# A two-block transformer kernel on one core: RMS norms by token on partitions, a weight split moved on VectorE, and a triangular inverse done two chunks at a time

## The reference, cut to what matters

```
def first_block(x, ...):                                   # 256 tokens, D 1024, D_FF 2816
    x = x + 0.5 * swiglu(rms_norm(x, ffn1_norm), ...)
    h = rms_norm(x, mix_norm);  p = h @ w_in
    y_a = rwkv7_mixer(token_shift(p[..., :SHIFT_COLS], mu), ...) @ rwkv_proj
    y_b = fox_mixer(...) @ fox_proj                        # forgetting attention, 8 heads of 64
    x = x + (gate_a * y_a + gate_b * y_b) @ w_out
    x = x + 0.5 * swiglu(rms_norm(x, ffn2_norm), ...)
    return rms_norm(x, final_norm)

def second_block(x, c, ctx, c_ctx, w_ada, ...):
    mod_x, mod_c = silu(c) @ w_ada + b_ada, silu(c_ctx) @ w_ada + b_ada     # 9 x 1024 each
    x   = x   + 0.5 * g1x * swiglu_2(modulate(rmsnorm(x), sh1x, sc1x), ...)
    ctx = ctx + 0.5 * g1c * swiglu_2(modulate(rmsnorm(ctx), sh1c, sc1c), ...)
    # both sets: projections, two-way retention; x: 2D rope, Fourier branch, gates, out
    x = x + g3x * 0.5 * swiglu_2(...)
    return rmsnorm(x, norm_final)
```

## Time and profile before

| | before |
|---|---|
| median of 3 runs | 1769.89 us (1769.77 to 1769.99) |
| the profiled execution | 1771.81 us |
| its span, first to last instruction | 1770.0 us |
| PE busy | 1704.9 us (96%) |
| DVE busy | 1059.6 us (60%) |
| ACT busy | 652.3 us (37%) |
| PE granted clock, mean | 0.991 of full |

### The profile page before, as it was taken

The page is one execution under the profiler, slowest core; times in us unless marked ns, Lnnn a source line. Parts: engine busy times, 40 slices in busy tenths (PEclk is TensorE's granted clock), DMA queues, the critical chain, the costliest instruction groups (busy, mean ns, idle before and its releaser), DMA issues.

```text
span 1770.0 us, 32228 instructions
## 1 busy us (share of the span) xinstructions
PE 1704.9 (96%) x13366; PEld 1552.1 (88%) x13366; DVE 1059.6 (60%) x1570; ACT 652.3 (37%) x763; POOL 5.2 (0%) x13
## 2 busy tenths in 40 slices
PE   6999999899999999999999999899999999999997
PEld 6999898676998999998888888888889799989997
DVE  6766747542766766765465465942356634676766
ACT  4333446222544333432222212522346334443332
POOL 0000000000000000000000000000000000000000
PEclk9999999999999999999999999999999999999999
DMA  6545566476244545422222222232223235445551
GB/s 245 190 175 185 193 257 240 152 283 256 100 165 171 190 168 187 166 85 105 95 95 95 95 95 96 95 119 104 90 96 106 97 143 185 176 151 184 185 190 48
DMA packets 37537, 267.74 MB, mean 151 GB/s; under 512 B 4192, under 2 KB 4448, under 8 KB 5456
## 3 DMA queue, kind: packets, MB, share of 16 engines
q1 hardware_dynamic: 36432, 262.37, 40.8%
q0 software_dynamic: 1024, 4.17, 0.6%
HBM read 265.48 MB, written 1.05 MB: 151 GB/s over the span
## 4 chain that ended last, share of the span: by engine, by line
PE 92%; DVE 4%; ACT 2%; issue 1%; DMA 1%; DVEq 0%; POOL 0%; SPq 0%; ACTq 0%
PE PS L329 25%; PE PS L330 24%; PE PS L331 24%; PE PS L542 2%; PE PS L543 2%; PE PS L544 2%; PE PS L562 2%; PE PS L981 2%; PE PS L407 1%; PE PS L1014 1%; PE PS L1001 1%; ACT W_HI L316 1%; PE PS L783 1%; DVE RSTD L1467 1%; PE PS L968 1%
## 5 line engine op out<-in xcount | busy, mean ns | idle before, releaser
L329 PE MATMUL PS<-H_HI,W_HI 128*128 128x256 f32 (+1 forms) x2128 | 652.0, 306 | 21.0 <-DVE H_LO L1459 11.9
L330 PE MATMUL PS<-H_LO,W_HI 128*128 128x256 f32 (+1 forms) x2128 | 647.0, 304 | 0.0
L331 PE MATMUL PS<-H_HI,W_LO 128*128 128x256 f32 (+1 forms) x2128 | 646.8, 304 | 0.0
L316 ACT ACTIVATE W_HI<-RAW 128x2048 fp32r<-128x2048 f32 x213 | 407.2, 1912 | 585.0 <-PE PS L331 553.9
L324 DVE TENSOR_TENSOR W_LO<-RAW,W_HI 128x2048 fp32r<-128x2048 f32 x213 | 487.3, 2288 | 189.4 <-ACT W_HI L316 188.9
L329 PEld LDWEIGHTS PS<-H_HI,W_HI 128*128 128x128 f32 x2128 | 411.2, 193 | 43.8 <-issue 27.6
L330 PEld LDWEIGHTS PS<-H_LO,W_HI 128*128 128x128 f32 x2128 | 411.5, 193 | 15.4 <-issue 0.2
L331 PEld LDWEIGHTS PS<-H_HI,W_LO 128*128 128x128 f32 x2128 | 411.1, 193 | 14.9
L329 PE MATMUL PS<-HID_HI,W_HI 128*128 128x256 f32 (+1 forms) x704 | 218.4, 310 | 3.3 <-DVE XC L1509 3.3
L330 PE MATMUL PS<-HID_LO,W_HI 128*128 128x256 f32 (+1 forms) x704 | 217.9, 309 | 0.0
L331 PE MATMUL PS<-HID_HI,W_LO 128*128 128x256 f32 (+1 forms) x704 | 217.8, 309 | 0.0
(11 more groups left out here) (315 smaller groups left out, 1713.8 us busy)
## 6 DMA issues: line engine op xcount, KB each, us to landing
RAW<-stream SPq DMA_DIRECT2D x249, 1024.0 KB, 4.8
XC<-xin SPq DMA_DIRECT2D x2, 512.0 KB, 5.0
XC<-xin POOLq DMA_DIRECT2D x1, 1024.0 KB, 5.1
out<-NT POOLq DMA_DIRECT2D x2, 512.0 KB, 2.9
CON<-consts POOLq DMA_DIRECT2D x1, 548.0 KB, 6.0
LW<-lora POOLq DMA_DIRECT2D x1, 512.0 KB, 6.6
DFT<-dft POOLq DMA_DIRECT2D x1, 512.0 KB, 3.8
ROPE<-rope POOLq DMA_DIRECT2D x1, 256.0 KB, 3.4
```

What stands on the lines that cost most here:

```text
L316: nc.scalar.activation(W_HI[s % RING][:], RAW[u % RING][:], ACT.Copy).then_inc(hi_done, 1)
L329: nc.tensor.matmul(acc, w_hi, x_hi, start=first, stop=False)
L330: nc.tensor.matmul(acc, w_hi, x_lo, start=False, stop=False)
L331: return nc.tensor.matmul(acc, w_lo, x_hi, start=False, stop=last)
```

## The change

1. **Norms.** The squares become the stationary operand (tokens on the result's partitions) and a two-column constant `ONE3` the moving one, so the sums are 128x2. The root and the reciprocal are of 128x2, and `norm_spread` brings the reciprocals back to every partition with a matmul against the identity; DVE scales from PSUM. All eight tiles are scaled first, and then all are subtracted. PE's first unit takes the high activations first (`two`), and the low ones behind. `nd` and `ne` share one pass over the squares: a second column of weights `SQW` gives the sum for the norm behind the norm.
2. **Order on DVE.** `split_lo(s0 + 34)` leaves the end of the FFN: it goes behind the additions, in two halves, or, ahead of the FFN of both sets, ahead of the reciprocals of `nd`. The first norm's low split moves between the scaling and the subtraction.
3. **PE fill.** Seven matmuls at the start, and three to five around the norms `na`, `nc` and `ni` (`keep_clock`), compute nothing that is used.
4. **The end of the FFN of both sets** is done by set: eight tiles of the main set, eight of the context, each 256 columns wide instead of eight of 512. The norm `ng` runs beside the context's tiles.
5. **The inverse in pairs of chunks.** The odd chunk of a pair has its heads' halves crossed, so it uses the two 64x64 tiles off the diagonal. One `z_step` and one `x_step` stand for two. In `x_step` the products with `ZM` on the left stay on the diagonal for both chunks, and those of the odd chunk wait for a semaphore `x_cross`. `products` of odd chunks has another order. `ada(12)` ahead becomes `ada(16)`, twenty `ada(4)` become ten `ada(8)`, and `ada(12)` ahead of `fox_qk` becomes two times `ada(4)`.
6. The output is stored by SP in four pieces instead of by GpSimd in two.

`three` also takes the high, the low and again the high weights instead of high, high, low. That leaves the number of matmuls and weight loads as it is.

How the change moves the instructions stands here at two places, engine by engine in program order.

```diff
-ADA_INV = 23
-ADA_AFTER = {PHASE["fox_qk"] - 1: 3, PHASE["fox_v"] + 1: ADA_INV}
+ADA_INV = 24
...
+            o = slice(0, UNIT) if part is None else slice(part * UNIT // 2, (part + 1) * UNIT // 2)
+            last = nc.vector.tensor_tensor(W_LO[s % RING][:, o], RAW[u % RING][:, o], W_HI[s % RING][:, o].bitcast(F32), ALU.subtract)
+            if part != 0:
+                last.then_inc(lo_done, 1)
...
-                last = nc.tensor.matmul(NORM_BANK[name], con("ones"), tmp[:, k], start=(k == 0), stop=(k == 7))
-                if k == 7:
+                w = 4 if name == "nd" else 2
+                for tt in range(2):
+                    last = nc.tensor.matmul(sums(name), tmp[:, k, tt * P:(tt + 1) * P], SQW[:, k, 2 - 2 * tt:6 - 2 * tt] if w == 4 else
...
+            def keep_clock(n, bank):
+                for _ in range(n):
+                    nc.tensor.matmul(BK8[bank][:, 0:ROWS], con("ident"), CON[:, 0:ROWS], start=True, stop=True)
+            def norm_spread(name):
+                pe.wait_ge(S("norm_rec"), NORM[name] + 1)
+                for q in ((2, 3, 0, 1) if name == "nd" else (0, 1)):
+                    last = nc.tensor.matmul(spread_of(name)[:, q * P:(q + 1) * P], RSTD[:, q:q + 1].to_broadcast([P, P]), con("ident"),
+                                            start=True, stop=True)
+                last.then_inc(S("norm_spread"), 1)
...
+                    if t == 0 and f == 0:
+                        for k in range(KT):
+                            pe.wait_ge(S("norm_hi"), KT * NORM_H[h_name] + k + 1)
+                            for w in range(2):
+                                c = (w * KT + k) * P
+                                nc.tensor.matmul(tile(w), W_HI[sl][:, c:c + P], H_HI[:, 0, k], start=(k == 0), stop=False)
+                        wait_unit(s, j, j0)
+                        for w in range(2):
+                            for k in range(KT):
+                                c = (w * KT + k) * P
+                                nc.tensor.matmul(tile(w), W_LO[sl][:, c:c + P], H_HI[:, 0, k], start=False, stop=False)
...
+                    for q, t in ([(q, 0) for q in range(4)] + [(q, 1) for q in range(4)] +
+                                 [(q, t) for q in range(4, 16) for t in range(2)]):
+                        h, m = q // 8, q % 8
+                        if q < 4:
+                            if q == 0:
+                                pe.wait_ge(S("hid_lo"), f * FT + FT - 1 + t)
+                            if t == 0:
+                                pe.wait_ge(S("down_added"), d + q - 3)
+                        elif t == 0 and q < 12:
+                            pe.wait_ge(S("main_added"), q - 3)
+                        elif t == 0:
+                            pe.wait_ge(S("down_added"), d + q - 11)
+                        c = (t * KT + m) * P
+                        last = three(BK8[4 + q % 4][:, 0:ROWS], W_HI[sl][:, c:c + P], W_LO[sl][:, c:c + P],
+                                     HID_HI[:, t, h * ROWS:(h + 1) * ROWS], HID_LO[:, t, h * ROWS:(h + 1) * ROWS], t == 0, t == 1)
+                        if t == 0:
+                            continue
+                        last.then_inc(psum_ready if h else S("main_down"), 1)
+                        if q == 9:
+                            norm(then)
+                        if q == 11:
+                            norm_spread(then)
...
+                    pe.wait_ge(S("sqw"), 1)
                     up_ctx(0)
-                    norm(h_name)
-                    up_ctx(1)
+                    up_ctx(1, (0,))
+                    norm_spread("nd")
+                    up_ctx(1, (1,))
...
+            pe.wait_ge(S("warm_in"), 1)
+            for _ in range(7):
+                nc.tensor.matmul(BK8[0][:, 0:ROWS], WARM[:, 0:P], WARM[:, P:P + ROWS], start=True, stop=True)
+            pe.wait_ge(S("one3"), 1)
+            for k in (6, 7, 0):
+                norm_sum("na", k, first=6, last_k=0)
             pe.wait_ge(S("con_in"), 16)
-            norm("na")
+            keep_clock(1, 0)
+            norm_spread("na")
+            keep_clock(2, 0)
             ffn(0, "ffn1", 1, "na", "nb")
-            ada(12)
+            ada(4)
+            norm_spread("nb")
+            ada(4)
...
+                for i in range(IT):
+                    o = slice(i * CH, (i + 1) * CH)
+                    for p0 in (0, CH):
+                        nc.tensor.matmul(BK8[2][p0:p0 + CH, o], TTNK[p0:p0 + CH, c, 0, i], X2[p0:p0 + CH, c, 0, i], start=True, stop=True)
+                    for p0 in (0, CH):
+                        last = nc.tensor.matmul(BK8[3][CH - p0:P - p0, o], TTNK[p0:p0 + CH, c + 1, 0, i], X2[p0:p0 + CH, c + 1, 0, i],
                                                 start=True, stop=True)
                 last.then_inc(S("z"), 1)
...
+                for i in range(IT if lev < 5 else 0):
+                    o = slice(i * CH, (i + 1) * CH)
                     for p0 in (0, CH):
-                        if lev < 5:
...
+                        nc.tensor.matmul(BK8[4][p0:p0 + CH, o], X2[p0:p0 + CH, c, 1, i], ZM[p0:p0 + CH, c, i], start=True, stop=True)
+                    for p0 in (0, CH):
+                        last = nc.tensor.matmul(BK8[5][CH - p0:P - p0, o], X2[p0:p0 + CH, c + 1, 1, i], ZM[p0:p0 + CH, c + 1, i],
+                                                start=True, stop=True)
+                if lev < 5:
+                    last.then_inc(S("x_cross"), 1)
+                for d in range(2):
+                    if d and lev < 5:
+                        pe.wait_ge(S("x_cross"), n + 1)
+                    for i in range(IT):
+                        for p0 in (0, CH):
+                            last = nc.tensor.matmul(BK8[4 + d][p0:p0 + CH, ROWS + i * CH:ROWS + (i + 1) * CH], ZM[p0:p0 + CH, c + d, i],
+                                                    X2[p0:p0 + CH, c + d, 1, i], start=True, stop=True)
                 last.then_inc(S("x"), 1)
...
+                z_first(c)
+            ada(16)
+            z_step(0)
+            for n in range(10):
                 x_step(n)
-                if n + 2 < 6 * NC:
-                    z_step(n + 2)
-                if k % 2 == 0 and h < NH:
-                    if h + 1 < NH:
-                        scores(h + 1)
-                    turn_probs(h)
-                if k % 2 and h < NH:
-                    values(h)
-                ada(4)
+                if n < 9:
+                    z_step(n + 1)
+                if n < NH:
+                    if n + 1 < NH:
+                        scores(n + 1)
+                    turn_probs(n)
+                ada(8)
+                if n < NH:
...
-                split_lo(dve, s0 + 34)
-                add(10, range(8), m0 + 124)
+                if halves == 1:
+                    add(10, range(8), m0 + 124)
...
+            split_lo(dve, PHASE["fox_qk"] + 1, part=0)
+            reciprocal("nb")
+            split_lo(dve, PHASE["fox_qk"] + 1, part=1)
+            norm_rows("nb", 0, lambda k: par("nm", k))
...
+            ctx_add(0)
+            ctx_add(1)
+            split_lo(dve, PHASE["ret_q"] + 1, part=0)
+            reciprocal("ng")
+            ctx_add(2)
+            ctx_add(3)
+            dve.wait_ge(S("norm_spread"), NORM["ng"] + 1)
+            for k in range(KT):
+                scale("ng", 0, k, lambda k: GAIN[:, 2, k:k + 1], NT)
+                if k % 2:
+                    ctx_add(4 + k // 2)
+            for k in range(KT):
+                rest("ng", 0, k, (24, 0))
+            split_lo(dve, PHASE["ret_q"] + 1, part=1)
```

377 lines of the change are left out of this document (244 added, 133 removed).

## The result

The changed kernel took **1755.27 us** (median of 4, 1751.69 to 1757.49), the one before 1769.83 beside it: ratio 0.9918, 95% interval [0.9901, 0.9935]. It is faster by 0.8%, 14.6 us, where 26 were forecast, and 1.3 us outside the range.

The account below looks back on a forecast made before the run. PE was taken to bound the kernel, busy for 96% of the span. Terms summed to -26.0 us against the profiled 1771.81, giving 1745.8, and 1744 for the median, 1.92 lower; range 1734 to 1754.

Parts of the forecast that it names:

- The inverse, -4.0: Inverse with its products: pair steps gain 8.5 us, less load waits, added unit, longer products and clock; net -4.0 us.
- the wait of 2.9 us in `ada(16)`: Ahead of the pair steps: PE stands 2.9 us for RAW, because `ada(16)` needs a fourth unit.
- the clock's fall behind it: Just behind `ada(16)`: PE's clock at 0.5 for 3 to 7 us.
- the waits at the end: End of the inverse: two steps with `ada(8)` want four units in 7 us; a load takes 2.45, the ring holds three.
- stepped through pair by pair, the stage of 77.8 becomes some 73: Inverse stage: 77.8 us becomes some 73, after which `products` take 0.9 of the gain back.
- the inverse gives nothing: Rival at the inverse: `ada(16)` wait, clock fall in it and slow loads cancel the gain; 1748 to 1750 us, chance 0.2.
- The added 0.9 in the odd products: `products` of the two odd chunks: three groups where two stood, costing 0.9 us.
- First FFN to `fox_qk`, -4.0: Between these places: late-addition wait goes (1.65), a shorter chain is covered by `ada(8)`, one `ada` unit moves out; -4.0 us.
- costed at two spreads: At `nf`: two spreads more, +0.4 us.
- The clock at `nc`, `ng`, `ni`: At these norms: clock 1.00, held by matmuls between; at `nc` 2.3 us had been lost to the lower clock.
- the terms of 4.6 and 2.5: FFN of both sets to `ret_q`, -4.6 us; second FFN to the FFN of both sets, -2.5 us.
- Start and end: Start: second unit starts earlier, -4.4 us. End: shorter chain and earlier last store, -2.3 us.

## Why the prediction was wrong

**The inverse, -4.0: the step that failed.** The count of instructions was right, and the gain by it even low: the two double steps took 2.0 us where 1.88 were worked out, a pair with its head took 6.7 to 7.1 us where the loop ran freely (forecast 7.07), and without loads pairs are worth 10.5 us. Also right: the wait of 2.9 us in `ada(16)` (3.2 measured), the clock's fall behind it, the waits at the end. What failed is the sentence "stepped through pair by pair, the stage of 77.8 becomes some 73". It charged loads only where PE would stand in front of one. But the stage ran at a DMA share of 0.76 before, with PE almost always busy, so it was close to two bounds at once. When PE's work shrank by some 7 us, the idle time grew by as much, from 5.0 to 12.9. Waits for RAW went from 3.5 to 5.9, waits without a releaser, which I read as late instructions, from 0 to 4.5, and the lower clock behind such idle time (0.97 of 81.5 us) cost some 2 us more. The rival "the inverse gives nothing" had the right place and 0.2; it named the first wait, the fall and slow loads, not the instructions, and its 1748 to 1750 was too low since other terms failed too. The added 0.9 in the odd products cannot be told: from the first copy of BKR to the first soft-max are 17.0 us before, 17.4 and 17.2 after, but 18.2 in the kernel before with pairs and 18.0 to 18.6 in the changed kernel with the old products.

**First FFN to `fox_qk`, -4.0.** The chain behind the sums of `nb` was to take 2 us where 4.09 stood. From the last sum (209.81) to the first product (213.94) it took 4.13, at a mean clock of 0.59 (first row of the stretches above), so 2.4 at full level. So 1.7 us went to a fall that I had placed at four other norms and not here, where I counted `ada` as cover. With wide matmuls in the gap ahead the stretch is 1.4 shorter. The other 1.2 are a longer wait for the squares (1.4, where 0.8 stood) and two spreads of PE's own time, about 0.5, which the sum counted as covered. The same fall stands at `nf`, which I had costed at two spreads (+0.4, measured +1.6).

**The clock at `nc`, `ng`, `ni`** held in both traces of the changed kernel, as forecast, and its price was right: 2.3 us forecast at `nc`, 2.4 measured by filling the gap in the kernel before. The rest of these terms, the shorter chain, gave nothing at `nc` or `ni`: the extra sums and matmuls fill what the chain gave up. At `ng` and ahead of the FFN of both sets, where the change takes work away (the second chain, the wait behind the last unit), the terms of 4.6 and 2.5 came as 4.3 and 3.1. Start and end were within 0.6.

**Sums** of 2 columns were taken at 0.235 us, from the row with 8 columns. The six at `nb`, two records each, took 1.50, so 0.25:

```profile
208.31 1.50 PE L427 MATMUL PS<-ONE,NT 128*128 128x2 f32 x12 [1.36 <-DVE NT L1623]
```

The Trainium skill, page "TensorEngine Tiling (Array Packing)", section "Instruction Overhead", would have them at about a tenth of that, an estimate from its 60 cycles for a matmul at 2.4 GHz; the row decides against it, as the earlier trace rows had said. The same page of the Trainium skill, section "Gotcha 1: PSUM Pressure", says that different row tiles cannot use one PSUM bank at the same time. This trace does not agree: both halves of the rows wrote one bank in the pair steps, and they overlapped (16 products in 0.52 us).

**The median.** The sum was made against one execution, and I moved it by 1.9 to the median. For the changed kernel that step is wrong by itself: its first trace shows 18.1 us of gain at a clock of 0.994, its second 11.3 at 0.989, and the median of its ten executions stands at 0.9925, where before has 0.994 beside the second trace. So the change seems to make falls somewhat more frequent as well as moving them; that short idle times and narrow matmuls are the reason is my reading.

## What to carry to other kernels

Where PE is almost always busy in a stage whose DMA share is as high as here (0.75 to 0.79), do not book shorter matmul work as gain: here 10.5 us of it gave 0 to 6. Moving five of the 24 loads out did not bring it back (2 to 3). Leave the loads out once, with constants in their place, and the two times show what there is to gain before anything is rewritten. Look at the stage's idle time and at "issue" in the waits: many small matmuls beside a full queue of loads may run out of instructions. And ahead of shortening a chain between two wide stretches, fill its gap with wide matmuls and measure that: at two norms here it gave, in the traces, all that the rewritten norm gave.

## What the runs showed of the hardware

- **Instructions come by DMA, and PE waits behind their packets.** The profile lists packets of 16 KB on a queue of kind "instruction", some 6 to 7 us apart in a stage full of small matmuls. PE stood up to 3.1 us with no releaser, and each of the 27 stalls over 1 us ended 1.2 to 1.5 us behind such a packet, 26 of them beside loads. Without loads the longest were 1.2 and 0.96 us. That the packets come late because of the loads is the reading that fits; it was not shown apart. I had not expected this; "issue" had looked like noise of the trace.
- **The clock falls at places with a probability.** Ten executions of the same program had mean granted clocks from 0.987 to 0.995, and their times, 1751.7 to 1763.0 us, follow it. Counted over the eighteen traces: behind `nb` with the new narrow sums it fell in 9 of 11 traces, and in none of the 4 with wide matmuls in the gap; at `nf` in 8 of 11, and none of 4; at `nc` in 6 of 15 with wide matmuls there (for 3.4 us, once 6.8) and in all 3 without (3.4 to 10.2 us); at `ni` in 2 of 15, and in all 3. Wide matmuls in an idle time make a fall rarer and mostly shorter; they do not exclude it.
- **Four 64x64 tiles in float32** overlap, crossed and diagonal ones mixed, and with both row halves writing one bank: 16 products on four tiles took 0.52 us, 16 on the two diagonal ones 0.86 to 0.94.
